# Two weight sums of the feed-forward, from VectorE additions to accumulating DMAs that GpSimd issues

## The chip, the cores and the metric

The kernel runs on one core of a Trainium2 chip. Its metric is the device time of one execution in microseconds (us). Before the change it is 2135.71 us, the median of 3 runs (2135.28 to 2136.56).

## The reference

One encoder layer in float32: a sequence of 512 tokens, width 2048, 16 heads of 128, feed-forward width 5632. Only the first mixer is used, since the depth is 1.

```python
h = rmsnorm(x, mix_norm_g)
x = x + forgetting_attention(h, w_in, b_f, g_q, g_k, w_out)
h = rmsnorm(x, ffn_norm_g)
gu = jnp.einsum('bsd,df->bsf', h, w_gate_up)          # (512,2048) x (2048,11264)
gate, up = gu[..., :D_FF], gu[..., D_FF:]
x = x + jnp.einsum('bsf,fd->bsd', jax.nn.silu(gate) * up, w_down)   # (512,5632) x (5632,2048)
```

## The kernel before

The first part of the kernel makes the attention. The change does not touch it. From about 833 us on the feed-forward runs.

**Seven products in place of eight.** The feed-forward cuts every large product into 2x2 blocks and computes them with seven block products (the Strassen-Winograd scheme). The activations' sums are kept in `a_form`. The weights' sums T1 to T4 have to be made for each tile of weights, after it is loaded. Each float32 operand is split into a high part and a rest (`f_hi`, `f_lo`), and every block product is three matmuls: high by high, high by rest, rest by high.

**Rounds and units.** The work is a list of 264 units, `UNITS`, each a triple (r, g, j). There are 17 rounds r: 11 for gate and up (one for each 512 of the 5632 hidden columns) and 6 for the down projection. Each round has a first pass (g=0) and a second pass (g=1), with 8 units each in the rounds 0 to 12 and 7 in the rounds 13 to 16. A unit takes 256 rows of weights (two halves r of 128 partitions each, apart in memory) by two column groups c of 512.

- A unit of the first pass loads three blocks of 128x512 (768 KB), and TensorE makes three products of it, 18 matmuls.
- A unit of the second pass loads all four blocks (1 MB, two DMAs of 512 KB). TensorE makes four products of it, 24 matmuls. Half of the units, 132, are of this kind. Before the matmuls the sums are made in place in the raw tile `f_raw`: blocks 0 and 1 become T1 and T3 by adding blocks 1 and 3 to them, then block 3 becomes T4 (block 0 + block 3), then block 2 becomes T2 (block 3 + block 2).

**Four slots and their chain.** `f_raw` has four slots, unit n uses slot n % 4. `f_lo` lies over the same bytes, `f_hi` has three slots. The chain of one unit of the second pass is: SyncE waits until TensorE is done with unit n-4 (`unit_done`) and issues the loads (`f_ld`), VectorE makes T1 and T3 (`sums_t1_t3`, L1436), then T4 and T2 (`sums_t2_t4`, L1441 and L1443), ScalarE copies the first two blocks to `f_hi` when T1 and T3 are there (`weights_hi`, L1023) and the last two when T2 is (`weights_hi_rest`, L1060), VectorE subtracts to make `f_lo` (`weights_lo`, L1391, or in two halves `weights_lo_halves`, L1449), and TensorE waits for `f_lo_done` before the unit's first matmul (L765).

**The order on the engines** is written out by hand. While TensorE works on unit n, VectorE makes `f_lo` of unit n+1 and the sums of unit n+2, and behind them the other work of the round: reading the products out of PSUM, the hidden values, the sums of their forms, the rests of the forms loaded for the down projection (L1506). `lo_first` decides whether T1 and T3 of unit n+2 stand before or behind `f_lo` of unit n+1: they stand behind it at the last two units of a first pass and at the first unit of a second pass. ScalarE makes `f_hi` of unit n+2 during unit n. GpSimd has nothing to do in the feed-forward but a norm at its start and two additions at its end. SyncE's queue also carries the loads of the stored forms (L394) in the down projection, and ScalarE's the stores of the forms (L1140).

Of the kernel before, what the change touches and what calls it, by code (L numbers as in the profile page):

```python
# [27 lines left out]
P = 128  # L28
F32 = mybir.dt.float32
F32R = mybir.dt.float32r  # L30
ALU = mybir.AluOpType
# [7 lines left out]
def encoder_layer(nc, x, mix_g, ffn_g, w_in, b_f, g_q, g_k, w_out, w_gu, w_down, y):  # L39
# [8 lines left out]
    CW = 512  # L48
# [23 lines left out]
    FIRST = [0, 8, 15]  # L72
    R_DOWN = NP
# [2 lines left out]
    BASE = [sum(2 * k for k in ROUND_K[:r]) for r in range(NR + 1)]  # L76
    UNITS = [(r, g, j) for r in range(NR) for g in range(2) for j in range(ROUND_K[r])]
    NU = len(UNITS)
    LANDED, HI_COUNT, T_COUNT = [], [], []
    in_slot, his, ts = [0] * 4, 0, 0  # L80
    for n, (r_, g_, j_) in enumerate(UNITS):
        in_slot[n % 4] += 32
        LANDED.append(in_slot[n % 4])
        T_COUNT.append(ts)
        his += 1 + g_
        ts += g_
        HI_COUNT.append(his)
# [7 lines left out]
    with ctx:  # L95
        def at(name, offset, shape, dt=F32):
            return nc.alloc_sbuf_tensor_at(name, shape, dt, offset=offset)

        def sem(name):
            return ctx.enter_context(nc.semaphore(name))  # L100
# [39 lines left out]
        f_raw = at("f_raw", AREA_W, [P, 4, 4, CW])  # L140
# [95 lines left out]
        aform_hi, aform_lo = sem("aform_hi"), sem("aform_lo")  # L236
        rms2_done = sem("rms2_done")
        f_ld = [sem(f"f_loaded{s}") for s in range(4)]
        t_step, f_hi_done, f_lo_done = sem("t_step"), sem("f_hi_done"), sem("f_lo_done")
        unit_done, product_done = sem("unit_done"), sem("product_done")  # L240
        p1_read, p2_read, p3_read = sem("p1_read"), sem("p2_read"), sem("p3_read")
# [52 lines left out]
        for k, (_, add, (r_, g_, j_)) in enumerate(PIECES):  # L294
            PIECE_ADD[add] = k
            PIECE_LOAD[BASE[r_] + g_ * ROUND_K[r_] + j_] = k

        def early_piece(k):

            return rows[:, 1 + k // 2 * 2, k % 2 * 2:k % 2 * 2 + 2]  # L300
# [17 lines left out]
                SPLIT_NTH[s] = len(SPLIT_NTH)  # L318
        assert len(SPLIT_NTH) == 2 * NSTEP

        block = ctx.enter_context(nc.Block())


        @block.sync
        def _(sp):
# [45 lines left out]
            def store_x1(d):  # L371
                sp.wait_ge(bank_free, B_OUT + NT * (d + 1))
                sp.dma_start(dram_x1[d], rows[:, d]).then_inc(x1_stored[d], 16)
# [8 lines left out]
                if d > 0:  # L382
                    store_x1(d - 1)

            w_gu_v = w_gu.rearrange("(g r i p) (c x) -> g i p r c x", r=2, i=2, p=P, c=2)
            w_down_v = w_down.rearrange("(g r i p) (c x) -> g i p r c x", r=2, i=2, p=P, c=2)

            def load_forms(b, g, j):
                step = FIRST[b] + j
                sp.wait_ge(forms_stored[step % 2], 16 * (step // 2 + 1))  # L390
                if g == 0:
                    sp.dma_start(a_raw[j][:, 0:3], dram_forms[step][:, 0:3]).then_inc(first_ld[j], 16)
                else:
                    sp.dma_start(a_raw[j][:, 3:7], dram_forms[step][:, 3:7]).then_inc(second_ld[j], 16)  # L394

            for n in range(NU):
                r, g, j = UNITS[n]
                s = n % 4
                if n in (0, 1):
                    sp.wait_ge(w_lo_done, 2 * (U_OUT + 15 + n))  # L400
                elif n in (2, 3):
                    sp.wait_ge(slot_done, 4 * (U_OUT + 13 + n))
                else:
                    sp.wait_ge(unit_done, n - 3)
                if r < R_DOWN:
                    src, col = w_gu_v[j // 2, j % 2], r * CW
                else:
                    step = FIRST[(r - R_DOWN) // 2] + j
                    src, col = w_down_v[step // 2, step % 2], (r - R_DOWN) % 2 * CW
                if g == 0:  # L410
                    sp.dma_start(f_raw[:, s, 0:2], src[:, :, 0, col:col + CW]).then_inc(f_ld[s], 16)
                    sp.dma_start(f_raw[:, s, 2], src[:, 1, 1, col:col + CW]).then_inc(f_ld[s], 16)
                else:
                    for half in range(2):
                        sp.dma_start(f_raw[:, s, 2 * half:2 * half + 2], src[:, half, :, col:col + CW])\
                            .then_inc(f_ld[s], 16)
                if n == 3:
                    store_x1(ND - 1)
                for which in LOAD_AT.get(n - 4, []):
                    load_forms(*which)  # L420

                if n in PIECE_LOAD:
                    k = PIECE_LOAD[n]
                    d, half = PIECES[k][0]
                    src = dram_x1[d][:, 2 * half:2 * half + 2]
                    if k == 0:
                        for m in range(ND):
                            sp.wait_ge(x1_stored[m], 16)
                        for i in range(2):
                            sp.wait_ge(forms_stored[i], 16 * NP)  # L430
                    if k < 3:
                        sp.dma_start(early_piece(k), src).then_inc(early_ld[k], 16)
                    elif k < 7:
                        sp.wait_ge(piece_added, k)
                        sp.dma_start(x1_piece[:], src).then_inc(piece_ld, 16)
                    else:
                        sp.wait_ge(x1_p2, 4)
                        sp.dma_start(p2_kept[:], src).then_inc(last_piece_ld, 16)
# [28 lines left out]
        def _(pool):  # L467
            g = nc.gpsimd
# [79 lines left out]
            inv_rms(2, 3, signals=rms_done)  # L548
            pool.wait_ge(rms_done, 2)
            g.tensor_scalar(rms_neg[:], rms_x[:], -1.0, None, ALU.mult).then_inc(rms2_done, 1)  # L550

            for t in range(2):

# [293 lines left out]
        def _(act):  # L847
# [161 lines left out]
            def weights_hi(n):  # L1009

                r, g, j = UNITS[n]
                if n < 2:
                    act.wait_ge(slot_done, 4 * (U_OUT + 15 + n))
                elif n == 2:
                    act.wait_ge(aform_lo, 6)
                else:
                    act.wait_ge(unit_done, n - 2)
                if g == 0:
                    act.wait_ge(f_ld[n % 4], LANDED[n])
                    a.activation(f_hi[:, n % 3, 0:3], f_raw[:, n % 4, 0:3], ACT.Copy).then_inc(f_hi_done, 1)  # L1020
                else:
                    act.wait_ge(t_step, 3 * T_COUNT[n] + 1)
                    a.activation(f_hi[:, n % 3, 0:2], f_raw[:, n % 4, 0:2], ACT.Copy).then_inc(f_hi_done, 1)  # L1023

            for d in range(ND):
# [30 lines left out]


            def weights_hi_rest(n):
                act.wait_ge(t_step, 3 * T_COUNT[n] + 3)
                a.activation(f_hi[:, n % 3, 2:4], f_raw[:, n % 4, 2:4], ACT.Copy).then_inc(f_hi_done, 1)  # L1060

            def read_p1_p2(r):
# [79 lines left out]
            def down_forms_hi(b, g, j):  # L1142
                act.wait_ge((second_ld if g else first_ld)[j], 16 * (b + 1))
                forms = slice(3, 7) if g else slice(0, 3)
                a.activation(a_form[:, j, 0, forms], a_raw[j][:, forms], ACT.Copy).then_inc(down_hi, 1)

            weights_hi(1)
            x1_squares(ND - 1, 3)
            for n in range(NU):
                r, g, j = UNITS[n]  # L1150
# [7 lines left out]
                if n + 2 < NU:  # L1158
                    weights_hi(n + 2)
                if n + 2 < NU and UNITS[n + 2][1] == 1:  # L1160
                    weights_hi_rest(n + 2)
# [33 lines left out]
        def _(dve):  # L1195
            v = nc.vector
# [191 lines left out]
            def weights_lo(n):  # L1388
                g = UNITS[n][1]
                dve.wait_ge(f_hi_done, HI_COUNT[n])  # L1390
                v.tensor_tensor(f_lo[:, n % 4, 0:3 + g], f_raw[:, n % 4, 0:3 + g],  # L1391
                                f32(f_hi[:, n % 3, 0:3 + g]), ALU.subtract).then_inc(f_lo_done, 1)
# [37 lines left out]
                        weights_lo(0)  # L1430


            def sums_t1_t3(n):
                dve.wait_ge(f_ld[n % 4], LANDED[n])
                f = f_raw[:, n % 4]
                v.tensor_tensor(f[:, 0:2], f[:, 0:2], f[:, 1:4:2], ALU.add).then_inc(t_step, 1)  # L1436

            def sums_t2_t4(n):
                f = f_raw[:, n % 4]
                dve.wait_ge(t_step, 3 * T_COUNT[n] + 1)  # L1440
                v.tensor_tensor(f[:, 3], f[:, 0], f[:, 3], ALU.add).then_inc(t_step, 1)  # L1441
                dve.wait_ge(t_step, 3 * T_COUNT[n] + 2)
                v.tensor_tensor(f[:, 2], f[:, 3], f[:, 2], ALU.add).then_inc(t_step, 1)  # L1443

            def weights_lo_halves(n):
# [205 lines left out]
            for n in range(NU):  # L1651
                r, g, j = UNITS[n]
                hidden = 1 <= r <= R_DOWN
                last = j == ROUND_K[r] - 1
                sums = n + 2 < NU and UNITS[n + 2][1] == 1
                lo_first = (g == 0 and j >= ROUND_K[r] - 2) or (g == 1 and j == 0)
                if sums and not lo_first:
                    sums_t1_t3(n + 2)
                if n + 1 < NU:
                    if lo_first and UNITS[n + 1][1] == 1:  # L1660
                        weights_lo_halves(n + 1)
                    else:
                        weights_lo(n + 1)
                if sums and lo_first:
                    sums_t1_t3(n + 2)
                if sums:
                    sums_t2_t4(n + 2)
                if g == 0:
# [89 lines left out]
```

## Time and profile before

| | |
|---|---|
| median of 3 runs | 2135.71 us |
| the profiled execution, its own time | 2136.44 us |
| its span, first to last instruction | 2134.7 us |
| TensorE busy in the span | 99% |
| VectorE busy in the span | 71% |
| feed-forward, 833 to 2125 us: TensorE busy | 1285.27 of 1292 us |
| the same stretch: VectorE busy | 1131.13 us |
| the same stretch: busy share of the 16 DMA engines | 0.69 |

The profile is of one execution. The time of the profiled execution is 1.74 us above its span (start and end around it). Busy time of an engine tells little here by itself: TensorE is busy nearly all the time because everything that a unit needs is ready when the unit before ends. What matters for a change is how much earlier than needed each tile of weights is ready, and that is read from the instructions in order of time.

### The profile page before, as it was taken

Reading aid. Unit: us, or ns where it says so; the run is one execution under the profiler, and the core shown is the slowest. Engines: PE = TensorE matmul, PEld = TensorE weight load, DVE = VectorE, ACT = ScalarE, POOL = GpSimd, SP = SyncE. Lnnn points to the kernel's source line nnn. Section 1 sums busy time; section 2 is a strip of 40 time slices with the busy share of each in tenths; the row PEclk is TensorE's granted clock in tenths of the full one; section 3 lists DMA queues with packets and bytes.
Section 4 is the critical chain, followed back from the end, with each engine's and each line's share of the span. In section 5 each row is a group of like instructions: output and inputs, shape, how many; then the busy total and the mean of one; then the engine's idle time right before and its main releaser. Section 6 shows DMA issues by size and latency. Waiting matters only on the chain. (4 is left out here: it accounts for less than half of the span.)

```text
span 2134.7 us, 27909 instructions
## 1 busy us (share of the span) xinstructions
PE 2113.3 (99%) x10404; PEld 1845.4 (86%) x10404; DVE 1526.2 (71%) x2108; ACT 944.6 (44%) x1281; POOL 174.2 (8%) x354
## 2 busy tenths in 40 slices
PE   8999999999999999999999999999999999999998
PEld 8999999999998888888888888888888777887876
DVE  4444444444455435888888987987978998999999
ACT  5333333333343335444444444544445554544533
POOL 0322222222221000000000000000000000000000
PEclk9999999999999999999999999999999999999999
DMA  6232333232243344666666666676677877868766
GB/s 185 76 99 79 93 85 92 79 98 79 84 128 128 119 134 132 198 218 200 219 212 211 208 219 212 204 233 204 198 235 232 269 256 246 263 208 269 260 186 203
DMA packets 258924, 376.31 MB, mean 176 GB/s; under 512 B 15842, under 2 KB 114180, under 8 KB 258324
## 3 DMA queue, kind: packets, MB, share of 16 engines
q1 hardware_dynamic: 255456, 354.90, 52.8%
q10 hardware_dynamic: 3380, 20.21, 2.5%
q8 instruction: 58, 0.95, 0.2%
q14 instruction: 30, 0.25, 0.0%
HBM read 346.45 MB, written 28.61 MB: 176 GB/s over the span
## 5 line engine op out<-in xcount | busy, mean ns | idle before, releaser
L1391 DVE TENSOR_TENSOR f_lo<-f_raw,f_hi 128x1536 fp32r<-128x1536 f32 (+1 forms) x230 | 454.4, 1980 | 46.9 <-ACT f_hi L1020 31.4
L564 PE MATMUL gemm<-w_hi,act_t 128*128 128x384 f32 (+2 forms) x1280 | 450.7, 352 | 2.3 <-DVE w_lo L1207 2.3
L565 PE MATMUL gemm<-w_lo,act_t 128*128 128x384 f32 (+2 forms) x1280 | 443.9, 347 | 0.0
L566 PE MATMUL gemm<-w_hi,act_t 128*128 128x384 f32 (+2 forms) x1280 | 443.9, 347 | 0.0
L765 PE MATMUL gemm<-f_hi,a_form 128*128 128x512 f32 x1056 | 411.2, 389 | 0.0
L767 PE MATMUL gemm<-f_hi,a_form 128*128 128x512 f32 x1056 | 411.1, 389 | 0.0
L766 PE MATMUL gemm<-f_lo,a_form 128*128 128x512 f32 x1056 | 410.8, 389 | 0.0
L765 PE MATMUL aux<-f_hi,a_form 128*128 128x512 f32 x792 | 313.2, 395 | 6.7 <-DVE f_lo L1391 5.1
L1207 DVE TENSOR_TENSOR w_lo<-w_raw,w_hi 128x768 fp32r<-128x768 f32 (+1 forms) x160 | 160.7, 1008 | 208.5 <-ACT w_hi L862 208.5
L766 PE MATMUL aux<-f_lo,a_form 128*128 128x512 f32 x792 | 308.5, 390 | 0.0
L767 PE MATMUL aux<-f_hi,a_form 128*128 128x512 f32 x792 | 308.5, 390 | 0.0
L1020 ACT ACTIVATE f_hi<-f_raw 128x1536 fp32r<-128x1536 f32 x132 | 196.2, 1486 | 202.3 <-DMA f_raw<-in_ffn_w_gate_up 84.7
L564 PEld LDWEIGHTS gemm<-w_hi,act_t 128*128 128x128 f32 x1280 | 240.9, 188 | 13.0 <-issue 2.7
L565 PEld LDWEIGHTS gemm<-w_lo,act_t 128*128 128x128 f32 x1280 | 241.1, 188 | 10.5
L566 PEld LDWEIGHTS gemm<-w_hi,act_t 128*128 128x128 f32 x1280 | 240.9, 188 | 10.0
L765 PEld LDWEIGHTS gemm<-f_hi,a_form 128*128 128x128 f32 x1056 | 198.2, 188 | 41.9 <-ACT rows L1101 0.4
L767 PEld LDWEIGHTS gemm<-f_hi,a_form 128*128 128x128 f32 x1056 | 198.2, 188 | 41.4
L766 PEld LDWEIGHTS gemm<-f_lo,a_form 128*128 128x128 f32 x1056 | 198.2, 188 | 41.2
L1060 ACT ACTIVATE f_hi<-f_raw 128x1024 fp32r<-128x1024 f32 x132 | 140.2, 1062 | 211.3 <-DVE f_raw L1443 211.3
L1023 ACT ACTIVATE f_hi<-f_raw 128x1024 fp32r<-128x1024 f32 x132 | 140.2, 1062 | 190.7 <-DVE f_raw L1436 187.4
L862 ACT ACTIVATE w_hi<-w_raw 128x768 fp32r<-128x768 f32 (+1 forms) x160 | 136.3, 883 | 187.8 <-PE gemm L566 187.8
L1436 DVE TENSOR_TENSOR f_raw<-f_raw 128x1024 f32<-128x1024 f32 x132 | 161.1, 1221 | 56.8 <-DMA f_raw<-in_ffn_w_gate_up 50.1
(184 smaller groups left out, 2227.5 us busy)
## 6 DMA issues: line engine op xcount, KB each, us to landing
f_raw<-in_ffn_w_gate_up SPq DMA_DIRECT2D x264, 512.0 KB, 4.2
f_raw<-in_ffn_w_down SPq DMA_DIRECT2D x132, 512.0 KB, 4.8
w_raw<-in_fox_w_in SPq DMA_DIRECT2D x192, 256.0 KB, 3.3
f_raw<-in_ffn_w_gate_up SPq DMA_DIRECT2D x88, 256.0 KB, 4.0
w_raw<-in_fox_w_out SPq DMA_DIRECT2D x16, 1024.0 KB, 5.1
f_raw<-in_ffn_w_down SPq DMA_DIRECT2D x44, 256.0 KB, 4.9
a_raw<-forms_scratch SPq DMA_DIRECT2D x22, 512.0 KB, 6.6
forms_scratch<-fa_a ACTq DMA_DIRECT2D x11, 896.0 KB, 6.3
```

The lines of the kernel that those rows point to most:

```text
L564: mm(out, a_hi, b_hi, start=first, stop=False)
L565: mm(out, a_hi, b_lo, start=False, stop=False)
L566: return mm(out, a_lo, b_hi, start=False, stop=last)
L765: mm(banks[t][:], st_hi, hi, start=j == 0, stop=False)
L766: mm(banks[t][:], st_hi, lo, start=False, stop=False)
L767: i = mm(banks[t][:], st_lo, hi, start=False, stop=j == ROUND_K[r] - 1)
L1020: a.activation(f_hi[:, n % 3, 0:3], f_raw[:, n % 4, 0:3], ACT.Copy).then_inc(f_hi_done, 1)
L1023: a.activation(f_hi[:, n % 3, 0:2], f_raw[:, n % 4, 0:2], ACT.Copy).then_inc(f_hi_done, 1)
L1060: a.activation(f_hi[:, n % 3, 2:4], f_raw[:, n % 4, 2:4], ACT.Copy).then_inc(f_hi_done, 1)
L1207: v.tensor_tensor(w_lo[:, j % 2, k, 0:width], w_raw[:, j % 2, k, 0:width], f32(w_hi[:, j % 2, k, 0:width]), ALU.subtract).then_inc(w_lo_do ...
L1391: v.tensor_tensor(f_lo[:, n % 4, 0:3 + g], f_raw[:, n % 4, 0:3 + g], f32(f_hi[:, n % 3, 0:3 + g]), ALU.subtract).then_inc(f_lo_done, 1)
L1436: v.tensor_tensor(f[:, 0:2], f[:, 0:2], f[:, 1:4:2], ALU.add).then_inc(t_step, 1)
```

## The change

The addition that makes T1 and T3 is taken off VectorE. In its place GpSimd waits for the loads of the unit (`f_ld`), and issues one DMA with `accum_op=ALU.add`: it reads the two blocks of column group 1 from the weights in memory again (512 KB) and adds them to blocks 0 and 1 of the slot. Its end raises `t1_t3` of that slot. ScalarE's copy of the first two blocks and VectorE's T4 wait for that semaphore. SyncE's loads stay as they were: all four blocks are still loaded.

```diff
+            for n in range(NU):
+                if UNITS[n][1] == 1:
+                    pool.wait_ge(f_ld[n % 4], LANDED[n])
+                    src, col = weights_of(n)
+                    pool.dma_start(f_raw[:, n % 4, 0:2], src[:, :, 1, col:col + CW], accum_op=ALU.add)\
+                        .then_inc(t1_t3[n % 4], 16)
...
                 else:
-                    act.wait_ge(t_step, 3 * T_COUNT[n] + 1)
+                    act.wait_ge(t1_t3[n % 4], SUMMED[n])
                     a.activation(f_hi[:, n % 3, 0:2], f_raw[:, n % 4, 0:2], ACT.Copy).then_inc(f_hi_done, 1)
...
-                act.wait_ge(t_step, 3 * T_COUNT[n] + 3)
+                act.wait_ge(t_step, 2 * T_COUNT[n] + 2)
...
-            def sums_t1_t3(n):
-                dve.wait_ge(f_ld[n % 4], LANDED[n])
-                f = f_raw[:, n % 4]
-                v.tensor_tensor(f[:, 0:2], f[:, 0:2], f[:, 1:4:2], ALU.add).then_inc(t_step, 1)
...
             def sums_t2_t4(n):
                 f = f_raw[:, n % 4]
-                dve.wait_ge(t_step, 3 * T_COUNT[n] + 1)
+                dve.wait_ge(t1_t3[n % 4], SUMMED[n])
                 v.tensor_tensor(f[:, 3], f[:, 0], f[:, 3], ALU.add).then_inc(t_step, 1)
-                dve.wait_ge(t_step, 3 * T_COUNT[n] + 2)
+                dve.wait_ge(t_step, 2 * T_COUNT[n] + 1)
                 v.tensor_tensor(f[:, 2], f[:, 3], f[:, 2], ALU.add).then_inc(t_step, 1)
...
-                if sums and not lo_first:
-                    sums_t1_t3(n + 2)
                 if n + 1 < NU:
                     if lo_first and UNITS[n + 1][1] == 1:
                         weights_lo_halves(n + 1)
                     else:
                         weights_lo(n + 1)
-                if sums and lo_first:
-                    sums_t1_t3(n + 2)
                 if sums:
                     sums_t2_t4(n + 2)
```

How VectorE's instructions stand at the start of the last round's second pass, before. L1436 is the addition that makes T1 and T3, L1441 and L1443 make T4 and T2, L1449 and L1391 make `f_lo` (of one unit):

```order
L1391 TENSOR_TENSOR f_lo<-f_raw,f_hi 128x1536
L1436 TENSOR_TENSOR f_raw<-f_raw 128x1024
L1441 TENSOR_TENSOR f_raw<-f_raw 128x512
L1443 TENSOR_TENSOR f_raw<-f_raw 128x512
L1449 TENSOR_TENSOR f_lo<-f_raw,f_hi 128x1024 x2
L1436 TENSOR_TENSOR f_raw<-f_raw 128x1024
```

The same place in the changed kernel, where the lines have moved (L1450 and L1452 make T4 and T2, L1458 and L1405 make `f_lo`):

```order
L1405 TENSOR_TENSOR f_lo<-f_raw,f_hi 128x1536
L1450 TENSOR_TENSOR f_raw<-f_raw 128x512
L1452 TENSOR_TENSOR f_raw<-f_raw 128x512
L1458 TENSOR_TENSOR f_lo<-f_raw,f_hi 128x1024 x2
L1450 TENSOR_TENSOR f_raw<-f_raw 128x512
```

T4 is now the first instruction that VectorE has for a unit of the second pass, and it stands directly behind the `f_lo` of the unit before.

In the middle of the same second pass VectorE's instructions stood so before:

```order
L1436 TENSOR_TENSOR f_raw<-f_raw 128x1024
L1391 TENSOR_TENSOR f_lo<-f_raw,f_hi 128x2048
L1441 TENSOR_TENSOR f_raw<-f_raw 128x512
L1443 TENSOR_TENSOR f_raw<-f_raw 128x512
L1519 TENSOR_TENSOR rows<-rows,p_kept 128x1024
L1436 TENSOR_TENSOR f_raw<-f_raw 128x1024
```

And so after the change:

```order
L1405 TENSOR_TENSOR f_lo<-f_raw,f_hi 128x2048
L1450 TENSOR_TENSOR f_raw<-f_raw 128x512
L1452 TENSOR_TENSOR f_raw<-f_raw 128x512
L1528 TENSOR_TENSOR rows<-rows,p_kept 128x1024
L1405 TENSOR_TENSOR f_lo<-f_raw,f_hi 128x2048
```

The `f_lo` of one unit no longer stands behind the addition of the unit after it. The work of the round (here L1519, in the changed kernel L1528) stands behind T4 and T2 in both.

The end of GpSimd's instructions in the changed kernel (L490 and L556 belong to the norm, L563 are the DMAs, L570 the last two additions). Before, no DMA stood between the norm's and the last two additions:

```order
L490 TENSOR_TENSOR rms_x<-mean_t,neg_half 128x4
L556 TENSOR_SCALAR rms_neg<-rms_x 128x4
L563 DMA f_raw<-in_ffn_w_gate_up 128x2x512 x88
L563 DMA f_raw<-in_ffn_w_down 128x2x512 x44
L570 TENSOR_TENSOR rows<-rows,p_kept 128x512 x2
```

GpSimd issues the 132 DMAs one after another in the order of the units, each behind its own wait.

## Rows read from the trace of the kernel before

**Rows 1.** Page, busy time, and the DMA queues of the whole span.

```profile
PE 2113.3 (99%) x10404; PEld 1845.4 (86%) x10404; DVE 1526.2 (71%) x2108; ACT 944.6 (44%) x1281; POOL 174.2 (8%) x354
...
q1 hardware_dynamic: 255456, 354.90, 52.8%
```

**Rows 2.** Feed-forward as one stretch: busy us and instructions per engine, clock, DMA share, GB/s.

```profile
833.00:2125.00 1292.00, 1285.27 (x5738) 1057.93 (x5737) 1131.13 (x1115) 620.90 (x648) 4.09 (x4) 1.00 0.69 224
```

**Rows 3.** Waits in the feed-forward: engine, line, waited for, us, times, longest.

```profile
PEld aux L765 <- DVE f_lo L1391: 12.2, 20, 1.8
PEld aux L765 <- DVE f_lo L1449: 3.0, 5, 1.0
```

**Rows 4.** Groups of VectorE in the feed-forward: count, busy us, mean ns, idle before.

```profile
L1436 DVE TENSOR_TENSOR f_raw<-f_raw 128x1024 f32<-128x1024 f32 x132 | 161.1, 1221 | 56.8 <-DMA f_raw<-in_ffn_w_gate_up 50.1 <-DMA f_raw<-in_ffn_w_down 6.2
```

**Rows 5.** Start of a second pass in order of time: start us, duration us.

```profile
1011.78 0.55 SPq L415 DMA_DIRECT2D f_raw<-in_ffn_w_gate_up  x1
...
1018.68 1.23 DVE L1436 TENSOR_TENSOR f_raw<-f_raw 128x1024 f32<-128x1024 f32 x1 [3.47 <-DMA f_raw<-in_ffn_w_gate_up]
...
1019.95 0.69 DVE L1441 TENSOR_TENSOR f_raw<-f_raw 128x512 f32<-128x512 f32 x1
1020.00 1.06 ACT L1023 ACTIVATE f_hi<-f_raw 128x1024 fp32r<-128x1024 f32 x1 [6.58 <-DVE f_raw L1436]
...
1021.28 2.44 DVE L1449 TENSOR_TENSOR f_lo<-f_raw,f_hi 128x1024 fp32r<-128x1024 f32 x2
...
1023.82 0.45 PE L765 MATMUL aux<-f_hi,a_form 128*128 128x512 f32 x1
```

**Rows 6.** Middle of the same second pass, one unit in order of time.

```profile
1040.53 0.54 SPq L415 DMA_DIRECT2D f_raw<-in_ffn_w_gate_up  x1
...
1046.13 1.22 DVE L1436 TENSOR_TENSOR f_raw<-f_raw 128x1024 f32<-128x1024 f32 x1 [0.64 <-DMA f_raw<-in_ffn_w_gate_up]
...
1049.47 0.69 DVE L1441 TENSOR_TENSOR f_raw<-f_raw 128x512 f32<-128x512 f32 x1
1050.19 0.69 DVE L1443 TENSOR_TENSOR f_raw<-f_raw 128x512 f32<-128x512 f32 x1
...
1050.92 1.06 ACT L1060 ACTIVATE f_hi<-f_raw 128x1024 fp32r<-128x1024 f32 x1 [2.41 <-DVE f_raw L1443]
...
1053.61 2.28 DVE L1391 TENSOR_TENSOR f_lo<-f_raw,f_hi 128x2048 fp32r<-128x2048 f32 x1
...
1056.65 0.39 PE L765 MATMUL aux<-f_hi,a_form 128*128 128x512 f32 x1
```

**Rows 7.** Issue to landing of the second pass's loads (L415), 512 KB each.

```profile
DMA to landing us min/median/max: 3.8/4.9/8.1
```

**Rows 8.** DMA issues of the page: count, KB each, median us to landing.

```profile
rows<-in_x SPq DMA_DIRECT2D x8, 1024.0 KB, 7.4
```

**Rows 9.** Second pass, 1023 to 1062 us, in 40 slices: DMA tenths, GB/s.

```profile
DMA  9748980069950279910689719979965984037950
GB/s 387 271 69 302 399 303 19 0 103 357 401 214 0 34 218 384 368 71 0 76 309 405 279 58 419 353 185 391 405 229 90 347 193 177 0 42 168 403 193 0
```

**Rows 10.** The last stretch: busy us per engine, granted clock, DMA share.

```profile
2050.00:2134.00 84.00, 75.50 (x332) 61.55 (x330) 79.15 (x78) 29.53 (x30) 2.95 (x2) 0.97 0.62 203
```

More of the change, by code:

```diff
@@ L78, in encoder_layer @@
     NU = len(UNITS)
-    LANDED, HI_COUNT, T_COUNT = [], [], []
-    in_slot, his, ts = [0] * 4, 0, 0
+    LANDED, HI_COUNT, T_COUNT, SUMMED = [], [], [], []
+    in_slot, in_sum, his, ts = [0] * 4, [0] * 4, 0, 0
     for n, (r_, g_, j_) in enumerate(UNITS):
@@ L83, in encoder_layer @@
         LANDED.append(in_slot[n % 4])
+        in_sum[n % 4] += 16 * g_
+        SUMMED.append(in_sum[n % 4])
         T_COUNT.append(ts)
@@ L238, in encoder_layer @@
         f_ld = [sem(f"f_loaded{s}") for s in range(4)]
+        t1_t3 = [sem(f"t1_t3_summed{s}") for s in range(4)]
         t_step, f_hi_done, f_lo_done = sem("t_step"), sem("f_hi_done"), sem("f_lo_done")
@@ L319, in encoder_layer, with weights_of @@
         assert len(SPLIT_NTH) == 2 * NSTEP
+        w_gu_v = w_gu.rearrange("(g r i p) (c x) -> g i p r c x", r=2, i=2, p=P, c=2)
+        w_down_v = w_down.rearrange("(g r i p) (c x) -> g i p r c x", r=2, i=2, p=P, c=2)
+        def weights_of(n):
+            r, _, j = UNITS[n]
+            if r < R_DOWN:
+                return w_gu_v[j // 2, j % 2], r * CW
+            step = FIRST[(r - R_DOWN) // 2] + j
+            return w_down_v[step // 2, step % 2], (r - R_DOWN) % 2 * CW
         block = ctx.enter_context(nc.Block())
@@ L383, in _ @@
                     store_x1(d - 1)
-            w_gu_v = w_gu.rearrange("(g r i p) (c x) -> g i p r c x", r=2, i=2, p=P, c=2)
-            w_down_v = w_down.rearrange("(g r i p) (c x) -> g i p r c x", r=2, i=2, p=P, c=2)
             def load_forms(b, g, j):
@@ L404, in _ @@
                     sp.wait_ge(unit_done, n - 3)
[L405 to L409, printed above, removed]
+                src, col = weights_of(n)
                 if g == 0:
@@ L550, in _ @@
             g.tensor_scalar(rms_neg[:], rms_x[:], -1.0, None, ALU.mult).then_inc(rms2_done, 1)
+            for n in range(NU):
+                if UNITS[n][1] == 1:
+                    pool.wait_ge(f_ld[n % 4], LANDED[n])
+                    src, col = weights_of(n)
+                    pool.dma_start(f_raw[:, n % 4, 0:2], src[:, :, 1, col:col + CW], accum_op=ALU.add)\
+                        .then_inc(t1_t3[n % 4], 16)
             for t in range(2):
```

## The prediction

> **What bounds the kernel now.** I read the page first: TensorE is busy for 99% of the span, VectorE for 71% [rows 1]. The change touches only the feed-forward, so I took that as one stretch. TensorE is busy there for 1285.27 of 1292 us at a granted clock of 1.00, VectorE for 1131.13, and the 16 DMA engines for 0.69 of the time [rows 2]. Next the list of waits of the same stretch. TensorE's weight load waits for `f_lo`, 12.2 + 3.0 = 15.2 us in 25 places, and for hardly anything else [rows 3]. So there is nearly nothing to win: the reader is to see that TensorE sets the pace, and that what comes closest to holding it back is the chain that ends in `f_lo`. What a longer chain costs is read last, from the instructions of single units in order of time, at the start and in the middle of a second pass [rows 5, 6].
>
> **What is removed.** 132 additions of 1.22 us, 161.1 us of VectorE [rows 4]. VectorE does not set the end, so this counts only by the 15.2 us for which TensorE waits on it. Part of those waits come from loads that land late, which the change leaves. I take half back, 7.6 us. The bounds are 0 and 15.2.
>
> **What is added.** 132 DMAs, each of which fetches 512 KB again and adds it to what lies in the slot. Call X the time from the landing of the loads to the landing of the accumulation: GpSimd's wake-up, its making of the descriptors, the transfer, the report. Before, this link of the chain was VectorE's 1.22 us. X enters the chain of each unit whole, because ScalarE's first copy and VectorE's T4 both wait for it, and T2, the second copy and `f_lo` follow from T4.
>
> *Start of a second pass* [rows 5]. The load of the unit is issued at 1011.78, is there at 1018.68, 6.90 us later, T4 starts at 1019.95, and the two halves of `f_lo` end at 1021.28 + 2.44 = 1023.72, 3.77 us behind T4's start. TensorE starts the unit at 1023.82. The room is 1023.82 - 1011.78 = 12.04 us, since only three short units of the first pass stand between slot and start. After the change the chain is 6.90 + X + 3.77 = 10.67 + X. TensorE waits X - 1.37 us.
>
> *Middle of a second pass* [rows 6]. The load is issued at 1040.53 and there by 1046.13, 5.60 us. T4 and T2 last from 1049.47 to 1050.88, 1.41. The copy takes 1.06, `f_lo` 2.28, and the hand-overs about 0.04 and 0.10. The chain is 5.60 + X + 1.41 + 1.06 + 2.28 + 0.14 = 10.49 + X. TensorE starts the unit at 1056.65, so the room is 16.12 us, and the loss X - 5.63, if X is above that.
>
> How often does each loss fall? With four slots, the first unit of the second pass starts late by X - 1.37. The next three were released before it and run behind it without a gap. The fifth waits for the slot of the first, one chain after its end, and so loses X - 5.63. The sixth to eighth follow without a gap, and the first pass after it has the room that this one lacked. So a round loses both once, (X - 1.37) + (X - 5.63) = 2X - 7.0, or X - 1.37 alone where X is below 5.63. There are 17 rounds, those with 7 units lose the same.
>
> **How large is X?** The trace has no accumulation and no DMA that GpSimd issues. The same 512 KB as a plain load take 3.8 us at the least, 4.9 in the median and 8.1 at the most from issue to landing [rows 7]. An accumulation has to read the slot as well as the weights, so it handles the bytes of two such loads. A plain load of 1 MB took 7.4 us [rows 8]. The low end is 3.8 us (it is as cheap as the fastest plain load), the high end two such loads one after the other, 2 x 4.9 = 9.8. I take 7.4: the row with the same bytes handled, and about the middle of the ends. It also falls into company: the next unit's loads are issued just when it starts, and the DMA engines are full in bursts of up to 419 GB/s with gaps between them [rows 9].
>
> The Trainium skill bears on this in "Collectives: The Full Stack", section "Why ReduceScatter is half of AllGather": a DMA that adds is slower because it needs two source reads, not because the addition costs time, and runs at about half the rate. No run here shows it yet. By that rule the 2 x 4.9 or 7.4 us rows are the right neighbours, by an addition that rides along free the 4.9 us row.
>
> The loss is 17 x (2 x 7.4 - 7.0) = 17 x 7.8 = 132.6 us. With the 7.6 us back it is 125 us. On the profiled execution, 2136.44 us in all with a span of 2134.7, this makes 2261.4, and as its time is 0.7 us above the median, 2260.7: I say 2261 us. By the ends of X: at 3.8, 17 x 2.43 = 41 us, and at 9.8, 17 x 12.6 = 214 us.
>
> **What is queued behind the new waits.** On VectorE, T4 waits for the accumulation, and behind it stand the additions of the round and, in the down projection, the rests of the forms (L1506). On ScalarE, the first copy of a unit waits, and behind it at the start of a second pass the reading of the third product (`read_p3`), for which TensorE's fourth product of the second pass waits. Both take as long as the unit's own chain takes and not longer, so I cost them at nothing while X is below 10. VectorE has the freed 161.1 us to make good on them. On GpSimd, a late DMA holds up the next one, but three units of the second pass take 16.12 us, 5.4 each [rows 6], and its queue has nothing else. Its last two additions come after TensorE's last unit, far behind the last DMA. SyncE's queue keeps its order.
>
> **Rivals.**
>
> *The accumulation is cheap.* X between 3.8 and 5.6. The middle of the pass then hides it, and only the start of each round pays: 41 to 17 x 4.23 = 72 us, less up to 7.6: 2169 to 2208 us. For it: the gaps in the DMA engines' time, 8 of the 40 slices are at 0 or 1 tenth [rows 9]. Against it: GpSimd has to make the descriptors first, and the slot must be read. "DMA: Bandwidth & Descriptors", section "Anatomy of one DMA — SWDGE (gpsimd) path", of the Trainium skill gives a DMA issued by GpSimd 2.0 us plus its bytes at 436 GB/s, an estimate of 3.2 us for 512 KB; by that figure the loss would be 17 x 1.83 = 31 us. No run here shows it.
>
> *The DMA engines fill up.* They are busy for 0.69 x 1292 = 891 us of the feed-forward [rows 2]. The 132 accumulations are 69.2 MB. Queue q1 moved 354.90 MB in 52.8% of 2134.7 us, that is 315 GB/s while busy [rows 1], so one pass over 69.2 MB is 220 us and two are 440. 891 + 440 = 1331 us would still fit into 1292 + 125 = 1417. If an accumulated byte costs three times a plain one, 891 + 660 = 1551 us is more than that, the loads land late too, and the feed-forward is 259 us longer: 2395 us. The same end comes if the descriptors of one accumulation take GpSimd several us, with X at 11: 17 x 15 = 255 us. For it: the down projection has the forms' loads beside the weights, and the engines are fullest there.
>
> *Not slower.* The accumulation ends within 1.37 us plus the slack that VectorE's relief gives, and TensorE's 15.2 us of waits go: 2121 us at best. The place is the start of each second pass, and the deciding point X = 1.37 us, as shown above. Against it stands every row of a DMA of that size, the fastest being 3.8 us. That the change does not do what it says (VectorE's line stays, or the accumulations aren't waited for) has nothing for it in the order of the instructions.
>
> A smaller matter: the granted clock is 1.00 over the feed-forward and 0.97 in the last stretch, where TensorE is busy for 75.5 of 84 us [rows 2, 10]. Waits of 6 us at the start of each pass could cost some clock as well. It is not in the sum.
>
> **How the numbers follow.** The forecast (X from 5.6 to 10) has 0.50, the cheap accumulation 0.20, full DMA engines or slow descriptors 0.25, not slower 0.05. About 0.2% is what a measurement here can tell from no change. Slower by more than that has 0.95, within it 0.02, faster 0.03. The range runs from 2185, in the cheap case, to 2400, just above the full DMA engines: outside are half of the cheap case, 0.05 of not slower, and the tail of the worst.
>
> **What will show it right or wrong.** In the changed profile, L1436 is gone and VectorE's busy time down by about 161 us. ScalarE's first copy and VectorE's T4 should name the accumulating DMA as what ended their idle time, with well over 100 us between them. TensorE's waits for `f_lo` should be near 140 us, two large ones in each round, at the first unit of a second pass (about 6 us) and the fifth (about 2 us), not spread evenly. The DMA share should be between 0.75 and 0.95. The landing time of the accumulations is X; if it is far from 7.4 us the size is wrong though the mechanism holds. If waits appear in first passes too, or the plain loads land much later than 4.9 us, it is the DMA engines that set the pace. If TensorE waits for products to be read rather than for `f_lo`, the queues behind the new waits were the mistake.

## The result, and the profile after

The changed kernel takes 2382.93 us, the median of 4 runs (2375.61 to 2384.96). Beside it the kernel before takes 2135.49. The ratio is 1.1145, with a 95% interval of 1.1131 to 1.1158: 11.5% slower, 247 us. The forecast was 2261 us, slower by 125, with a range of 2185 to 2400. The direction and the place were right, and the size was half of what came.

The feed-forward of the changed kernel as one stretch, with the same columns as [rows 2] (busy us and count of TensorE, its weight loads, VectorE, ScalarE and GpSimd, then granted clock, DMA share, GB/s):

```profile
833.00:2373.00 1540.00, 1358.83 (x5743) 1099.23 (x5742) 983.98 (x983) 620.51 (x650) 163.36 (x135) 0.95 0.83 233
```

It has grown from 1292 to 1540 us, by 248, so the whole loss is here. TensorE stands idle for 1540.00 - 1358.83 = 181.2 us of it, where it was 6.7. That is 174.5 us of new idle time. The other 73.5 us are in its busy time, 1358.83 against 1285.27, for the same matmuls. The clock tells why: 0.95 on average, where it was 1.00. VectorE is down by 147 us where the forecast said about 161: L1436 is gone and no other group changed by more than 0.6 us, but the records of neighbouring instructions overlap a little, so the 132 additions count for less in the engine's busy time than in their own sum. The DMA share is up from 0.69 to 0.83.

The waits of the same stretch (engine, line, what it waited for, us in all, times, longest), to set beside [rows 3]:

```profile
ACT f_hi L1037 <- DMA f_raw<-in_ffn_w_gate_up: 361.3, 85, 14.6
DVE f_raw L1450 <- DMA f_raw<-in_ffn_w_gate_up: 245.2, 72, 11.7
...
PE aux L779 <- DVE f_lo L1458: 91.4, 17, 8.2
...
PE aux L779 <- DVE f_lo L1405: 81.8, 33, 8.2
```

ScalarE's first copy (L1037) and VectorE's T4 (L1450) wait for the accumulation. L1458 makes `f_lo` at the start of a second pass, in two halves. TensorE waits for it 17 times, once in each round, 5.4 us each. L1405 is `f_lo` in the middle of a pass, 33 waits.

One start of a second pass, which answers to [rows 5]. L563 is GpSimd's DMA, its start stands for the moment at which the loads have landed (the small delay of GpSimd's own start so counts with the landing, and not with X):

```profile
1219.37 1.20 SPq L421 DMA_DIRECT2D f_raw<-in_ffn_w_gate_up  x2
...
1225.28 1.20 POOL L563 DMA_DIRECT2D f_raw<-in_ffn_w_gate_up  x1 [47.45 <-DMA f_raw<-in_ffn_w_gate_up]
...
1231.59 0.69 DVE L1450 TENSOR_TENSOR f_raw<-f_raw 128x512 f32<-128x512 f32 x1 [6.26 <-DMA f_raw<-in_ffn_w_gate_up]
...
1232.92 2.43 DVE L1458 TENSOR_TENSOR f_lo<-f_raw,f_hi 128x1024 fp32r<-128x1024 f32 x2
...
1235.41 0.50 PE L779 MATMUL aux<-f_hi,a_form 128*128 128x512 f32 x1 [3.83 <-DVE f_lo L1458]
```

The load lands after 5.91 us, X is 1231.59 - 1225.28 = 6.31 us, and TensorE waits 3.83. The fifth unit of the same pass, beside [rows 6]:

```profile
1243.20 1.26 SPq L421 DMA_DIRECT2D f_raw<-in_ffn_w_gate_up  x2
...
1249.74 1.20 POOL L563 DMA_DIRECT2D f_raw<-in_ffn_w_gate_up  x1 [7.95 <-DMA f_raw<-in_ffn_w_gate_up]
...
1258.31 0.69 DVE L1450 TENSOR_TENSOR f_raw<-f_raw 128x512 f32<-128x512 f32 x1 [5.93 <-DMA f_raw<-in_ffn_w_gate_up]
...
1260.85 2.29 DVE L1405 TENSOR_TENSOR f_lo<-f_raw,f_hi 128x2048 fp32r<-128x2048 f32 x1 [1.12 <-ACT f_hi L1074]
...
1263.19 0.80 PE L779 MATMUL aux<-f_hi,a_form 128*128 128x512 f32 x1 [3.69 <-DVE f_lo L1405]
```

Here the load lands after 6.54 us, X is 8.57 and the rest 4.83, 19.9 us in all. The two waits per round, at the first unit and at the fifth, are the ones that the recurrence of four slots gave. Set against the list of units, the 33 waits at L1405 are 17 at the fifth unit, 64.4 us, and 16 others, 17.4 us: 14 at the sixth to eighth units, and two in first passes, 1.1 us together.

What stands behind the first of these waits, TensorE's matmuls in order of time:

```profile
1236.11 0.63 PE L781 MATMUL aux<-f_hi,a_form 128*128 128x512 f32 x1
1236.54 0.63 PE L779 MATMUL aux<-f_hi,a_form 128*128 128x512 f32 x1
...
1239.39 0.40 PE L780 MATMUL aux<-f_lo,a_form 128*128 128x512 f32 x1
1239.62 0.39 PE L781 MATMUL aux<-f_hi,a_form 128*128 128x512 f32 x1
```

For about 3 us behind a wait of 3.83 us they come 0.43 us apart (1236.11 to 1236.54), later 0.23 (1239.39 to 1239.62). The granted clock of that stretch, in the columns of [rows 2], is 0.50, the lower level of 1.2 GHz; afterwards it is 1.00, 2.4 GHz:

```profile
1235.90:1239.10 3.20, 3.20 (x10) 2.44 (x8) 0.63 (x1) 0.71 (x2) 0.62 (x1) 0.50 1.06 342
```

The accumulations' issue to landing, minimum, median and maximum, and their DMA queue over the whole span (packets, MB, share of 16 engines), with the columns of [rows 1]:

```profile
DMA to landing us min/median/max: 5.6/8.0/12.8
```

```profile
q0 software_dynamic: 35904, 69.21, 16.9%
```

q0 is GpSimd's queue. 16.9% of 2383.2 us are 403 us for 69.21 MB.

### The profile page after: what moved, and what is told of

The parts are those of the page before. It is cut to its first block and busy times, and to the rows that moved or that the text cites. A ratio compares the mean times of both kernels' runs of the same rounds, so it can differ in the third digit from the quotient of the medians.

```text
span 2383.2 us, 27909 instructions
## 1 busy us (share of the span) xinstructions
PE 2186.4 (92%) x10404; PEld 1886.4 (79%) x10404; DVE 1380.0 (58%) x1976; ACT 943.3 (40%) x1281; POOL 332.9 (14%) x486
## 3 DMA queue, kind: packets, MB, share of 16 engines
q0 software_dynamic: 35904, 69.21, 16.9%
## 5 line engine op out<-in xcount | busy, mean ns | idle before, releaser
L1405 DVE TENSOR_TENSOR f_lo<-f_raw,f_hi 128x1536 fp32r<-128x1536 f32 (+1 forms) x230 | 454.9, 1982 | 108.1 <-ACT f_hi L1074 77.2
L779 PE MATMUL aux<-f_hi,a_form 128*128 128x512 f32 x792 | 341.6, 431 | 174.1 <-DVE f_lo L1458 91.4
L1037 ACT ACTIVATE f_hi<-f_raw 128x1024 fp32r<-128x1024 f32 x132 | 140.0, 1061 | 582.6 <-DMA f_raw<-in_ffn_w_gate_up 361.3
L779 PEld LDWEIGHTS aux<-f_hi,a_form 128*128 128x128 f32 x792 | 161.9, 204 | 230.7 <-DVE f_lo L1458 98.5
L780 PE MATMUL aux<-f_lo,a_form 128*128 128x512 f32 x792 | 331.5, 419 | 0.0
L781 PE MATMUL aux<-f_hi,a_form 128*128 128x512 f32 x792 | 330.1, 417 | 0.0
L1450 DVE TENSOR_TENSOR f_raw<-f_raw 128x512 f32<-128x512 f32 x132 | 91.2, 691 | 386.9 <-DMA f_raw<-in_ffn_w_gate_up 245.2
L563 POOL DMA_DIRECT2D f_raw<-in_ffn_w_gate_up x88 | 106.1, 1206 | 854.5 <-DMA f_raw<-in_ffn_w_gate_up 845.3
```

The costliest lines, as they stand in the source:

```text
L563: pool.dma_start(f_raw[:, n % 4, 0:2], src[:, :, 1, col:col + CW], accum_op=ALU.add)\
L779: mm(banks[t][:], st_hi, hi, start=j == 0, stop=False)
L780: mm(banks[t][:], st_hi, lo, start=False, stop=False)
L781: i = mm(banks[t][:], st_lo, hi, start=False, stop=j == ROUND_K[r] - 1)
```

## The experiments

Two theories stood against each other, and later a third. *Chain*: the loss is the delay X, paid where the chain of a unit has no room. *Volume*: the DMA engines are full. *Clock*: the slower clock behind each wait is a cost of its own. "Before" is the kernel before in the same set of runs, 2138 to 2139 us.

| kernel | us | ratio to before, 95% interval |
|---|---|---|
| e1_plain | 2298.08 | 1.0735, 1.0710 to 1.0760 |
| e2_off_chain | 2173.88 | 1.0164, 1.0147 to 1.0181 |
| e3_first_only | 2272.05 | 1.0628, 1.0611 to 1.0646 |
| e4_warm | 2381.13 | 1.1130, 1.1111 to 1.1149 |
| e5_early | 2368.67 | 1.1084, 1.1043 to 1.1126 |
| e6_not_first | 2365.81 | 1.1072, 1.1037 to 1.1106 |
| e7_half | 2290.75 | 1.0713, 1.0689 to 1.0737 |
| e10_read_first | 2383.05 | 1.1128, 1.1096 to 1.1159 |
| e9_no_sum | 2125.09 | 0.9942, 0.9929 to 0.9956 |
| e8_lo_first | 2170.23 | 1.0153, 1.0139 to 1.0167 |
| e11_warm_read | 2385.06 | 1.1130, 1.1090 to 1.1170 |
| e12_first_warm | 2235.95 | 1.0467, 1.0439 to 1.0496 |

**e1_plain: the addition itself.**

```diff
-                    pool.dma_start(f_raw[:, n % 4, 0:2], src[:, :, 1, col:col + CW], accum_op=ALU.add)\
+                    pool.dma_start(f_raw[:, n % 4, 0:2], src[:, :, 1, col:col + CW])\
```

> The DMA that GpSimd issues copies in place of adding, so T1 and T3 hold other data; size, issue and waits stay as in the changed kernel. Chain theory (the loss is the delay X between landing of the loads and landing of the added DMA, paid at the first and the fifth unit of each second pass, with a drop of TensorE's clock behind each wait): the loss follows X. If the addition costs a second read, X falls from 8.0 to about 5.5 us and the waits from about 17 x (2 x 8.0 - 7.0) = 153 to 17 x 4.1 = 70 us, with clock in all about 2240 us. If issuing is what costs, X stays at 8.0 and the time at 2383. Volume theory (the DMA engines are full): with half the engine time for the added DMAs the loss of 247 us halves, about 2260 us, and the plain loads land in 4.2 and 4.8 us as before the change.

The DMAs of e1_plain, issue to landing, and its queue:

```profile
DMA to landing us min/median/max: 4.0/5.5/9.2
```

```profile
q0 software_dynamic: 19008, 69.21, 8.3%
```

Both theories missed, 2240 and 2260 us against 2298. From issue to landing it is 2.5 us less, and the loss fell from 247 to 160 us, so making the DMA add costs some 87 us of it. The engine time for the same bytes is 8.3% of 2299.1 us, 191 us, against 403: a factor of 2.1. A second read would make such a doubling. The issue on GpSimd took 0.72 us where the accumulation took 1.20. But even a plain copy on the chain loses 160 us, over twice what the chain theory gave it without the clock (70 us). TensorE waits 63.7 us at the first units, near those 70, and 51.5 us more in the middle of the passes, where the theory had nothing for an X of 5.5. The plain loads did not go back to 4.2 and 4.8 us either: they land in 4.7 and 5.4 us in the median, nearly as late as beside accumulations (4.8 and 5.5), so the traffic delays them even without the second read. Whether the same copy lands sooner when another engine issues it wasn't tried.

**e2_off_chain: the traffic without the chain.** The kernel before, with this beside it (each DMA waits for the one before it, and the last is waited for before the tile is used again):

```diff
+                if 1 <= r < R_DOWN and g_ == 1:
+                    if sent:
+                        pool.wait_ge(idle_dma, 16 * sent)
+                    pool.wait_ge(f_ld[n % 4], LANDED[n])
+                    pool.dma_start(junk_act[:], w_gu_v[j // 2, j % 2][:, :, 1, r * CW:r * CW + CW],
+                                   accum_op=ALU.add).then_inc(idle_dma, 16)
...
```

> The kernel before, with VectorE's additions in place, and beside it GpSimd's accumulating DMAs of 512 KB for the 80 second-pass units of the rounds 1 to 10, into an unused tile for which nobody waits. Chain theory: the traffic alone costs little, 0 to 20 us, 2135 to 2155 us. Volume theory: 80 of 132 accumulations cost 80/132 of 247 us, 150 us, about 2285 us.

Both missed. 80 accumulations that nobody waits for cost 35 us. The loads of gate and up land later, as the page's DMA issues show (count, KB, median us to landing; it was 4.2 before the change):

```profile
f_raw<-in_ffn_w_gate_up SPq DMA_DIRECT2D x264, 512.0 KB, 5.2
```

By that, traffic for all 132 is worth about 58 us, if the down projection behaves like the rest, which wasn't tried. It works through the chain as well: counted at the matmuls, TensorE's waits for `f_lo` rose from 6.4 to 28.7 us, and its busy time in the feed-forward by 16.9 us at a clock of 0.99. These two are 39 of the 44 us by which the profiled execution's span is longer, so this traffic costs time mainly by making the weights late, and by the slow clock behind the waits.

**e3_first_only: 17 of the 132.**

```diff
+    BY_DMA = [g_ == 1 and (j_ == 0) for r_, g_, j_ in UNITS]
...
-                if UNITS[n][1] == 1:
+                if BY_DMA[n]:
                     pool.wait_ge(f_ld[n % 4], LANDED[n])
```

VectorE makes the other sums, in the order of before.

> T1 and T3 come from the accumulating DMA only at the first unit (j=0) of each second pass, 17 of the 132; VectorE makes the others. Chain theory: each of the 17 pays X - 1.37 = 6.6 us and a part of the clock loss (74 us over 34 waits, 2.2 us each): 17 x 8.8 = 150 us, about 2285 us; less if X is shorter in lighter traffic, with X = 6 about 2250. Volume theory: 17 of 132 accumulations cost 17/132 of 247 us, 32 us, about 2167 us.

An eighth of the DMAs makes over half of the loss, 134 us. This decides for the chain against the volume as the main cause. It is not a share of the loss, though: with the other 115 alone (e6_not_first) nearly the whole loss stays. The feed-forward of e3_first_only:

```profile
833.00:2252.00 1419.00, 1322.76 (x5731) 1083.64 (x5731) 1109.47 (x1096) 620.36 (x648) 25.04 (x20) 0.96 0.66 210
```

TensorE is idle for 96.2 us (17 waits of together 91.1), and busy for 37.5 us longer than before. The accumulations took 5.9 us in the median in gate and up and 8.8 in the down projection, where the forms are loaded beside them. With these, 17 x (X - 1.37) is 11 x 4.5 + 6 x 7.4 = 94 us: the first term of the forecast holds.

**e4_warm, e10_read_first, e11_warm_read: clock and queue in the changed kernel.** e4_warm does this before the first unit of each second pass; e10_read_first moves ScalarE's `read_p3` ahead of `weights_hi(n + 2)`; e11_warm_read does both.

```diff
+                for _ in range(40):
+                    nc.tensor.transpose(bank_d[0][:, 0:P], ident[:], ident[:])
```

> The changed kernel, with 40 small transposes (about 4 us) into a free PSUM bank that TensorE does before it waits for the first unit of each second pass, so that it does not stand idle there. Clock theory: of the 74 us by which TensorE's busy time grew, the half that follows the 17 first waits comes back, 2346 us, and the granted clock of the feed-forward rises from 0.95 towards 0.98. If the loss is waiting alone and TensorE's longer busy time has another reason, it stays at 2383 us or gets slower by what the transposes overrun.

> The changed kernel with ScalarE reading the third product (read_p3) before it copies the second unit's T1 and T3, and not behind. TensorE waited for this reading 4.7 us in all. Queue theory: that is given back and not more, 2378 us. Nothing changes if the waits only move: 2383 us.

> The changed kernel with both edits, TensorE kept at work by 40 transposes before the first unit of each second pass, and ScalarE's reading of the third product moved ahead. The transposes alone kept the clock up at the first unit, but TensorE then waited 17 us for that reading and the time did not change. If that queue was what took the gain, the time falls by 17 to 30 us against the changed kernel, 2353 to 2366 us. If the chain of the later units takes it whatever comes first (they cannot start before their accumulation has landed), it stays within 5 us of 2383.

None moved the time by more than its interval. In e4_warm the transposes filled the wait at the first unit in most rounds of gate and up, its first products came without the slow clock, and TensorE stood before the fourth product instead, 17.0 us in 9 waits. In the down projection they were too few, 1.6 to 4.7 us of wait were left in each round. One such stand before the fourth product:

```profile
1151.69 0.72 PE L779 MATMUL gemm<-f_hi,a_form 128*128 128x512 f32 x1 [1.93 <-ACT h_top L1127]
```

That wait is ScalarE's reading of the third product, queued behind the copy of the second unit, which waits for its accumulation. With this reading moved ahead too, the time did not fall either, and TensorE's waits for `f_lo` in the middle of a pass were 92.6 us in place of 81.8. So in the changed kernel TensorE's speed at the first unit is not what counts: what it gains, it waits for later.

e4_warm also shows that the length of a wait alone does not tell whether the slow clock follows. Behind the 1.93 us above it was 0.50 for some 3 us. Behind this longer one, at the fifth unit of a pass, it stayed at 1.00:

```profile
1266.30 0.50 PE L779 MATMUL aux<-f_hi,a_form 128*128 128x512 f32 x1 [3.28 <-DVE f_lo L1417]
```

```profile
1266.40:1270.00 3.60, 3.60 (x16) 2.96 (x17) 1.52 (x3) 2.12 (x2) 1.25 (x2) 1.00 0.74 220
```

**e12_first_warm: the clock where no later unit waits.** e3_first_only with 32 such transposes in gate and up, 60 in the down projection.

> The kernel with the accumulating DMA at the first unit of a second pass only (2272 us, TensorE waits 95 us and is busy 38.6 us longer than before the change, at a granted clock of 0.96), with small transposes in TensorE's wait at the first unit: 32 in gate and up (3.6 us), 60 in the down projection (6.8 us). The later units are not held by an accumulation here. Clock theory (the longer busy time is the slower clock behind each wait, and where no later unit waits for its accumulation it is a cost of its own): the 38.6 us come back but for what the transposes overrun, 2235 to 2245 us, at a clock near 1.00. If the slower clock is hidden by something else here too: 2272 us.

```profile
833.00:2221.00 1388.00, 1367.13 (x6450) 1134.78 (x6449) 1109.92 (x1096) 620.83 (x650) 24.86 (x20) 1.00 0.67 215
```

The clock is 1.00 and 36 us come back, as the clock theory said, 2.1 for each of the 17 waits. The slow clock is a cost of its own where nothing else holds the next units. In the changed kernel, where their accumulations do, the same cure gave nothing back.

**e5_early: issue it sooner.**

```diff
-                            .then_inc(f_ld[s], 16)
+                            .then_inc((f_top, f_ld)[half][s], 16)
...
-                    pool.wait_ge(f_ld[n % 4], LANDED[n])
+                    pool.wait_ge(f_top[n % 4], SUMMED[n])
```

> The changed kernel, with GpSimd issuing the accumulation as soon as the first of the unit's two loads is there (its own semaphore), since it needs only that half. Chain theory: the second load lands 0.6 to 1.5 us behind the first, the accumulation goes out that much sooner and the first and fifth waits of 17 rounds shrink by it: 20 to 50 us, 2335 to 2360 us. If the DMA engines' rate is what holds the accumulation up (it lands when all bytes in flight are through), issuing earlier moves nothing: 2383 us.

14 us less, between the two forecasts. TensorE's wait at the first units did not shrink, it was 91.4 us in the changed kernel:

```profile
PE aux L780 <- DVE f_lo L1460: 96.9, 17, 9.0
```

In the middle of the passes the waits fell from 81.8 to 67.1 us, which is where the gain is. From issue to landing it was 8.1 us in the median, not shorter. That the earlier issue is eaten at the first unit by bytes still in flight fits this, and no run shows it.

**e6_not_first: all but the first unit.** As e3_first_only, with `j_ > 0`.

> The accumulating DMA for all units of a second pass but the first (115 of 132), VectorE makes T1 and T3 of the first. Recurrence of the chain with four slots: the second unit has 13.6 us of room for a chain of about 10.7 + 6.5 = 17.2 us and waits 3.6 in place of the first, the sixth takes the place of the fifth (about 3.7): 17 x 7.3 = 124 us of waits and about 60 us of clock, about 2320 us. If the waits were bound to the first unit alone, taking it out would give back 91 us and more: below 2290 us. Volume theory: 115 of 132, 2351 us.

17 us less, 2366 where the recurrence gave 2320. The loss did move on to the second unit's accumulation, but not the way that the recurrence says: TensorE stands before the first unit's fourth product, and most of the waiting for `f_lo` is still at the fifth unit, 51.1 us in 17, where the recurrence had the sixth. TensorE's waits for ScalarE in e6_not_first:

```profile
PE gemm L780 <- ACT h_top L1119: 40.7, 11, 6.4
PE gemm L780 <- ACT p_kept L1119: 25.2, 4, 9.3
PE gemm L780 <- ACT rows L1119: 14.5, 2, 8.5
```

These 80.4 us are waits for `read_p3` (L1119), in all 17 rounds. That reading stands behind the second unit's copy, which waits for its accumulation.

**e7_half: half the bytes.**

```diff
-                    pool.dma_start(f_raw[:, n % 4, 0:2], src[:, :, 1, col:col + CW], accum_op=ALU.add)\
+                    pool.dma_start(f_raw[:, n % 4, 0], src[:, 0, 1, col:col + CW], accum_op=ALU.add)\
```

> The accumulating DMA adds one block in place of two (256 KB, T1 alone); T3 is left out and is block 1 as loaded. If X is mostly bytes, it halves from 8 to about 4 to 5 us, and the loss from 247 to about 100 us, 2235 us. If X is mostly fixed (issue 1.2 us, and the way there and back), it falls by about 1 us only and the time to about 2330 us. The issue on GpSimd tells itself: 0.6 us if it goes by descriptors.

Issue to landing 4.0, 5.7 and 9.8 us, and 0.87 us on GpSimd. Neither all bytes nor all fixed, and the time, 2291 us, lies between the two forecasts: half the bytes take 2.3 us off 8.0, so by an estimate about 4.6 us are for bytes and 3.4 fixed. The DMAs of e1_plain and e7_half take about the same engine time (8.3% and 9.0% of the span), land after nearly the same time and lose nearly the same. From 5.6 to 8.0 us the loss rises by about 90 us, 38 for each us. The forecast's slope was 2 x 17 = 34 us; its constant was 90 to 100 us too low. The slope is not that of the delay alone, since the traffic of these runs halves with it, and no run has the shorter delay with the traffic kept.

**e9_no_sum and e8_lo_first: what VectorE's relief is worth.** Both start from the kernel before. e9_no_sum cuts the addition to one column, so T1 and T3 are left out:

```diff
-                v.tensor_tensor(f[:, 0:2], f[:, 0:2], f[:, 1:4:2], ALU.add).then_inc(t_step, 1)
+                v.tensor_tensor(f[:, 0:2, 0:1], f[:, 0:2, 0:1], f[:, 1:4:2, 0:1], ALU.add).then_inc(t_step, 1)
```

> The kernel before with VectorE's addition for T1 and T3 cut to one column of 512, so the sums are left out: what the relief of VectorE is worth with no DMA in its place. TensorE waits 15.2 us for f_lo. If half of that is owed to VectorE, 2128 us; if all, 2120 us; if the waits come from loads that land late, no change, 2135 us.

It saves 13 us, of 15.2 at most. This is the whole prize for taking T1 and T3 off VectorE, even if their making cost nothing. e8_lo_first drops the first of these two calls and makes the second unconditional:

```diff
-                if sums and not lo_first:
-                    sums_t1_t3(n + 2)
...
-                if sums and lo_first:
+                if sums:
                     sums_t1_t3(n + 2)
```

> The kernel before with VectorE making f_lo of the next unit always before T1 and T3 of the one after it, as the changed kernel's order is. In the middle of a second pass f_lo waited for the next unit's load behind that addition. If that order costs, up to 10 us are given back, 2126 us; but T1 and T3 come 2.3 us later, and if they are what is late, it is slower by up to 17 x 1 = 17 us, 2152 us.

32 us slower, beyond either forecast. T1 and T3 made behind `f_lo` come 2.3 us later, and TensorE waits for `f_lo` in the middle of the pass in 77 places:

```profile
PEld aux L765 <- DVE f_lo L1391: 48.9, 77, 0.8
```

No run pointed to a version that beats the kernel before, except by leaving the sums out.

## Why the prediction was right in direction and short in size

- *TensorE sets the pace, there is nearly nothing to win.* Right. The prize is 13 us (e9_no_sum). I took 7.6 back from a bound of 15.2.
- *The first unit of each second pass waits X - 1.37.* Right. Forecast 17 x 6.03 = 102.5 us, measured 91.4 in 17 waits. X was 6.31 in the gate and up pass shown, less than 7.4. In the down projection it was more: single waits there go to 8.2 us.
- *The fifth unit waits X - 5.63.* Right place, wrong size. Forecast 30.1 us, measured 64.4 in 17 waits, so 34 us too little. The chain of [rows 6] was taken with the load's landing of before, 5.60 us, and X = 7.4. In the pass shown they were 6.54 and 8.57, which makes 2.1 us more per round, 36 us in 17. e2_off_chain shows that such traffic alone makes the loads land later. The sum counted each accumulation as a delay and none as traffic. The other 17.4 us are in 16 waits where the recurrence left no gap.
- *"It is not in the sum"*: the clock. By the profile this is the largest term that was missing. 73.5 us of the 248 are TensorE's longer busy time. The forecast named the clock and left it unpriced. e12_first_warm prices it at 36 us for 17 lone waits; in the changed kernel itself it can't be taken off by itself (e4_warm, e11_warm_read).
- *What is queued behind the new waits costs nothing.* Nearly right for the changed kernel: 4.7 and 1.8 us of waits for `read_p3`. Wrong as a rule: it is covered by the wait of the first unit, and with that wait gone it is 80.4 us (e6_not_first).
- *X = 7.4.* Measured 8.0 in the median. At 34 us for each us this is 20 us. That 7.4 came so near is in part luck: it was taken from one row of 1 MB loads, and the same page has another, shown below this list, by which the middle of the pass would have paid nothing and the loss been 17 x 3.7 = 63 us. The rule of the Trainium skill, "Collectives: The Full Stack", section "Why ReduceScatter is half of AllGather", that a DMA which adds reads two sources and runs at about half the rate, holds here: the engines spent 403 us on accumulations and 191 us on the same bytes copied. The estimate of 3.2 us for a DMA issued by GpSimd, from the Trainium skill, "DMA: Bandwidth & Descriptors", section "Anatomy of one DMA — SWDGE (gpsimd) path", is too low for this kernel: the fastest plain one took 4.0 us, of which GpSimd's issue is 0.72, and the median 5.5.
- *The full DMA engines as a rival* gave 2395 us, nearest to what came, by another way. The share is 0.83, and e3_first_only loses 134 us at a share of 0.66. It is the right number for a reason that these runs bear out only in part: the traffic does make loads late (e1_plain, e2_off_chain), but it does not set the pace.

The other row of 1 MB loads on the page of the kernel before (count, KB, median us to landing), beside [rows 8]:

```profile
w_raw<-in_fox_w_out SPq DMA_DIRECT2D x16, 1024.0 KB, 5.1
```

The sum, by the changed profile: 91.4 + 81.8 us of waits for `f_lo`, 8 of other idle time, less the 6.7 of before, and 73.5 of slow clock, together 248. Of the 123 us that the forecast of 125 fell short, 49.5 are idle time and 73.5 the clock. How much of the 73.5 the chain would have taken as waits at full clock stays open; e4_warm and e11_warm_read say most of what falls at the first unit.

## What to carry to other kernels

Before an operation is moved from an engine that has time to spare to a DMA, compare its latency with the room of the tile that has the least, not with the busy share: here 1.2 us of VectorE became 8.0 us of chain, and a room of 12 us could not hold it. Where slots are recycled, a delay is paid again each time that the ring comes round, so work out the recurrence, and use the landing times as they will be under the new traffic. Price what TensorE does behind each wait as well as the wait.

## What the runs showed of the hardware that was not expected

- Behind some waits (1.93 us in e4_warm at 1151.69, 3.83 in the changed kernel) matmuls of 512 columns came 0.43 us apart for some 3 us, then 0.23 again. The length of the wait did not decide it: 3.28 us in e4_warm at 1266.30 left the clock at 1.00. In the feed-forward of the kernel before, no wait of the matmuls was longer than 1.3 us and the clock was 1.00. Small transposes in the gap kept it up (e12_first_warm).
- GpSimd's issue of a DMA depends on what it does: 0.72 us for a copy of 512 KB, 0.87 for an accumulation of 256 KB, 1.20 for one of 512 KB.
- An accumulation takes 2.1 times the engine time of the copy, and shows 35904 packets against 19008. The accumulation of half the bytes shows 19008 as well.
